# Storing the residual rows away to make room for a third gate and up buffer

## The reference

```
x = x + mix @ w_out                        # attention outputs, projected, added to the residual x
h = rms_norm(x, ln2)
# router: the best group of 8 experts by a softmax, in it the best 2 experts, two weights per token
y = sum over the token's two experts e of weight * (silu(h @ w_gate[e]) * (h @ w_up[e])) @ w_down[e]
x = x + y
out = rms_norm(x, ln_f)
```

## Time and profile before

| | |
|---|---|
| median of three runs | 2105.37 us |
| profiled execution, own time | 2101.73 us |
| its span in the trace | 2099.1 us |
| PE busy | 1821.9 us (87%) |
| DVE, ACT, POOL busy | 618.3, 474.5, 429.7 us |
| moved by DMA over the span | 527.22 MB, mean 251 GB/s |
| the chain that ended last, largest part | the load of `ht_region<-in_w_up`, 33% |

### The profile page before, as it was taken

How to read it: one execution, slowest core, us unless ns; L and a number is a source line. 1 busy time by engine, 2 the same in 40 slices (tenths; PEclk the granted TensorE clock), 3 DMA queues, 4 the chain that set the end, 5 groups by cost and what they waited for, 6 DMA issues and landing times. The chain is left out here.

```text
span 2099.1 us, 28102 instructions
## 1 busy us (share of the span) xinstructions
PE 1821.9 (87%) x11148; PEld 1276.7 (61%) x11148; DVE 618.3 (29%) x1464; ACT 474.5 (23%) x1008; POOL 429.7 (20%) x478
## 2 busy tenths in 40 slices
PE   6998999999999999999968888888888888888880
PEld 4877777777666666688845554555545555555550
DVE  4321224444666566601331111111111111111115
ACT  5222223323434443422301011011011110110102
POOL 2323333331000013244111111111111111111110
PEclk9999999999999999999979999999999999999995
DMA  9453223323221231143479999999999999999985
GB/s 277 119 137 102 63 79 81 77 64 79 53 51 41 71 121 41 41 152 101 168 316 424 425 427 425 425 425 426 426 425 424 426 425 425 423 424 422 421 352 243
DMA packets 190056, 527.22 MB, mean 251 GB/s; under 512 B 65650, under 2 KB 148850, under 8 KB 162074
## 3 DMA queue, kind: packets, MB, share of 16 engines
q1 hardware_dynamic: 171498, 509.18, 63.0%
q0 software_dynamic: 18480, 16.97, 2.4%
HBM read 530.38 MB, written 46.02 MB: 275 GB/s over the span
## 5 line engine op out<-in xcount | busy, mean ns | idle before, releaser
L873 PE MATMUL PJ<-ht_rounded,ring_rounded 128*128 128x512 f32 (+1 forms) x928 | 320.5, 399 | 4.9 <-ACT at_region L1267 4.9
L1150 PE MATMUL PJ<-at_region,ring_region 128*64 128x256 f32 x1024 | 263.6, 423 | 69.9 <-DMA at_region<-in_w_up 68.9
L1150 PE MATMUL PJ<-ht_region,ring_region 128*64 128x256 f32 x1024 | 236.3, 391 | 41.6 <-DMA ht_region<-in_w_up 41.6
L1151 PE MATMUL PJ<-at_region,ring_region 128*64 128x256 f32 x1024 | 264.3, 423 | 0.0
L1150 PEld LDWEIGHTS PJ<-at_region,ring_region 128*64 128x64 f32 x1024 | 154.0, 153 | 159.5 <-issue 101.5
L1151 PE MATMUL PJ<-ht_region,ring_region 128*64 128x256 f32 x1024 | 237.0, 391 | 0.0
L750 POOL TENSOR_TENSOR ring_rounded<-ring_region,ring_rounded 128x512 fp32r<-128x512 f32 x100 | 127.4, 1305 | 480.1 <-ACT ring_rounded L1212 480.1
L802 POOL DMA_INDIRECT y_scratch<-ring_region,s_idx x64 | 64.6, 1009 | 779.6 <-DVE ring_region L1824 765.2
L1150 PEld LDWEIGHTS PJ<-ht_region,ring_region 128*64 128x64 f32 x1024 | 142.0, 141 | 120.1 <-issue 70.9
L873 PEld LDWEIGHTS PJ<-ht_rounded,ring_rounded 128*128 128x128 f32 (+1 forms) x928 | 171.7, 189 | 53.7 <-issue 12.0
L1816 DVE TENSOR_TENSOR ring_region<-ring_region,PJ 64x256 f32<-64x256 f32 x64 | 27.1, 423 | 593.0 <-ACT ring_region L1419 593.0
(11 more groups left out here) (265 smaller groups left out, 2691.6 us busy)
## 6 DMA issues: line engine op xcount, KB each, us to landing
at_region<-in_w_gate SPq DMA_DIRECT2D x32, 2048.0 KB, 14.0
at_region<-in_w_down SPq DMA_DIRECT2D x32, 2048.0 KB, 21.5
at_region<-in_w_up SPq DMA_DIRECT2D x32, 2048.0 KB, 21.6
ht_region<-in_w_gate SPq DMA_DIRECT2D x32, 2048.0 KB, 15.4
ht_region<-in_w_up SPq DMA_DIRECT2D x32, 2048.0 KB, 22.8
x_region<-in_w_down SPq DMA_DIRECT2D x32, 2048.0 KB, 22.5
ring_region<-in_w_in SPq DMA_DIRECT2D x36, 1024.0 KB, 5.9
ring_region<-in_w_out SPq DMA_DIRECT2D x16, 1024.0 KB, 5.1
```

The source lines that it names most:

```text
L873: ins = mm(out, w[:, k, 0:width], h[:, k, :], start=k == 0 and i == 0, stop=k == KT - 1 and i == 2)
L1150: mm(GU[0:CAP, 0:D_EXPERT], x, gate[:, j, :], start=j == 0, stop=j == KT - 1)
L1151: ins = mm(GU[CAP:2 * CAP, 0:D_EXPERT], x, up[:, j, :], start=j == 0, stop=j == KT - 1)
```

## The change

Four things are done, all in the list that SP runs, with what the other engines must know of them.

- `x_sb` is stored to a new HBM scratch, one row tile of 1 MiB at a time, as soon as its last addition is done. The four stores stand ahead of `load_down(0, 0)` and the stores of h.
- MIX0 becomes a third gate and up buffer, used once: for expert 1, loaded after `load_up(0, 0)` and once x is stored. The HT0 buffer, which the logits free, takes gate and up of expert 2.
- From expert 3 on the two old buffers alternate as before, but with the parity exchanged: odd experts in AT0, even ones in HT0. The down buffers keep their parity. The loads of experts 3 and 4 are written out ahead of the loop.
- After the last weight load four loads bring x back into MIX0, and DVE waits for them (`x_again`) before the final additions.

PE's program takes the buffer and its count from `gate_up_place` and is otherwise the same. The passes after the first, which run only if an expert has more than 64 rows, keep the old scheme.

```diff
-        ex_w = [AT0 + 12 * KB, HT0]
+        ex_w = [AT0 + 12 * KB, HT0, MIX0]
...
-            sp.wait_ge(wo_ready, NT * NT)
+            for t in range(NT):
+                sp.wait_ge(wo_added, NT * (NT - 1) + t + 1)
+                sp.dma_start(x_dram[t * P:(t + 1) * P, :], x_sb[:, t, :]).then_inc(x_stored, 16)
             load_down(0, 0)
...
             load_up(0, 0)
+            sp.wait_ge(x_stored, 16 * NT)
+            load_gate(1, 2)
+            load_up(1, 2)
             sp.wait_ge(logits_ready, 1)
-            load_expert(1, 1)
+            load_down(1, 1)
+            load_gate(2, 1)
+            load_up(2, 1)
...
-            expert_loads(0)
+            for e in (3, 4):
+                sp.wait_ge(gu_done, 1 if e == 3 else 3)
+                load_gate(e, (e + 1) % 2)
+                load_up(e, (e + 1) % 2)
+                sp.wait_ge(down_done, e - 2)
+                load_down(e - 1, (e - 1) % 2)
+            sp.wait_ge(down_done, 3)
+            load_down(4, 0)
+            with sp.Fori(0, (E_ALL - 6) // 2) as i:
+                for b in range(2):
+                    sp.wait_ge(gu_done, i * 2 + (b + 4))
+                    nxt = bass.ds(i * 2 + (b + 5), 1)
...
+                    sp.wait_ge(down_done, i * 2 + (b + 4))
...
+            sp.wait_ge(gu_done, E_ALL - 2)
+            load_gate(E_ALL - 1, 0)
+            load_up(E_ALL - 1, 0)
+            sp.wait_ge(down_done, E_ALL - 2)
+            load_down(E_ALL - 1, 1)
+            for t in range(NT):
+                sp.dma_start(x_sb[:, t, :], x_dram[t * P:(t + 1) * P, :]).then_inc(x_again, 16)
...
+            def gate_up_place(c, i, b4, first):
+                if not first:
+                    return b4 % 2, c * PAIRS + i * 2 + (b4 // 2 - b4 % 2)
+                if b4 % 2 == 0:
+                    return 1, i * 2 + (b4 // 2 - 1)
+                return 0, i * 2 + b4 // 2
...
+                gu, held = place
...
-                pe.wait_ge(gu_in[b], k * 32 + 32)
+                pe.wait_ge(gu_in[gu], held * 32 + 32)
...
             dve.wait_ge(lnf_in, 16)
+            dve.wait_ge(x_again, 16 * NT)
```

More of the change, by code:

```diff
@@ L324, in hybrid_block_moe_kernel @@
         y_dram = nc.dram_tensor("y_scratch", [2 * T, D], F32, kind="Internal").ap()
+        x_dram = nc.dram_tensor("x_scratch", [T, D], F32, kind="Internal").ap()
         KB = 256
@@ L527, in hybrid_block_moe_kernel @@
         slot_of_ready, table_ready = sem("slot_of_ready"), sem("table_ready")
+        x_stored, x_again = sem("x_stored"), sem("x_again")
         xg_cleared, g_copied, s_copied = sem("xg_cleared"), sem("g_copied"), sem("s_copied")
@@ L530, in hybrid_block_moe_kernel @@
         scattered = [sem(f"scattered{b}") for b in range(RUN)]
-        gu_in = [sem(f"gu_in{b}") for b in range(2)]
+        gu_in = [sem(f"gu_in{b}") for b in range(3)]
         down_in = [sem(f"down_in{b}") for b in range(2)]
@@ L700, in expert_loads @@
                           .then_inc(down_in[b], 16)
-            expert_loads(0)
+            for e in (3, 4):
[10 more added lines that the diff above has]
+                    nxt = bass.ds(i * 2 + (b + 5), 1)
+                    sp.dma_start(ex_halves(b, 0), gate_rows[:, nxt]).then_inc(gu_in[b], 16)
+                    sp.dma_start(ex_halves(b, 1), up_rows[:, nxt]).then_inc(gu_in[b], 16)
+                    sp.wait_ge(down_done, i * 2 + (b + 4))
+                    sp.dma_start(ex_down[1 - b].rearrange("p k (a n) -> p a (k n)", a=1), down_rows[:, nxt, :])\
+                      .then_inc(down_in[1 - b], 16)
+            sp.wait_ge(gu_done, E_ALL - 2)
[5 more added lines that the diff above has]
+                sp.dma_start(x_sb[:, t, :], x_dram[t * P:(t + 1) * P, :]).then_inc(x_again, 16)
             sp.wait_ge(most_ready, 1)
@@ L1134, in turn_gathered, with expert @@
                 ins.then_inc(xg_transposed, 1)
-            def expert(c, i, b4, last):
+            def gate_up_place(c, i, b4, first):
[4 more added lines that the diff above has]
+                return 0, i * 2 + b4 // 2
+            def expert(c, i, b4, last, place):
                 e = c * E_ALL + i * RUN + b4
@@ L1140, in expert @@
                 Y = S[:, b, :, :]
-                gate = ex_gu[b][:, 0, :].rearrange("p (k n) -> p k n", k=KT)
-                up = ex_gu[b][:, 1, :].rearrange("p (k n) -> p k n", k=KT)
-                pe.wait_ge(gu_in[b], k * 32 + 32)
+                gu, held = place
+                gate = ex_gu[gu][:, 0, :].rearrange("p (k n) -> p k n", k=KT)
+                up = ex_gu[gu][:, 1, :].rearrange("p (k n) -> p k n", k=KT)
+                pe.wait_ge(gu_in[gu], held * 32 + 32)
                 pe.wait_ge(xT_a, e + 1)
@@ L1173, in expert, with expert_pass @@
                 ins.then_inc(down_done, 1)
-            def expert_pass(c):
+            def expert_pass(c, first):
                 turn_gathered(c * E_ALL, c * RUNS, 0)
                 for b4 in range(RUN):
-                    expert(c, 0, b4, False)
+                    expert(c, 0, b4, False, ((0, 0), (2, 0), (1, 0), (0, 1))[b4] if first else gate_up_place(c, 0, b4, first))
                 with pe.Fori(1, RUNS - 1) as i:
                     for b4 in range(RUN):
-                        expert(c, i, b4, False)
+                        expert(c, i, b4, False, gate_up_place(c, i, b4, first))
                 for b4 in range(RUN):
-                    expert(c, RUNS - 1, b4, b4 == RUN - 1)
+                    expert(c, RUNS - 1, b4, b4 == RUN - 1, gate_up_place(c, RUNS - 1, b4, first))
             pe.wait_ge(slots_ready, 1)
-            expert_pass(0)
+            expert_pass(0, True)
             pe.wait_ge(most_ready, 1)
@@ L1190, in _ @@
                 with pe.Fori(1, PASSES) as c:
-                    expert_pass(c)
+                    expert_pass(c, False)
             with pe.Else():
```

## The result

The changed kernel takes 2112.16 us, the median of ten runs (2110.42 to 2113.54), against 2105.11 us for the kernel before (ten runs, 2101.54 to 2108.39). The ratio is 1.0036, with a 95% interval from 1.0028 to 1.0045. So the change makes the kernel slower, by 7.05 us between the medians and by 7.6 us (6 to 9.5) as the ratio has it. The prediction was 2114 us and +10.5. The profiled executions have spans of 2099.1 and 2108.3 us, 9.2 us apart.

What follows compares the result with a forecast made beforehand. Weight loads were taken to bound the expert stage, at 5.18 us per 2 MiB load. The terms -0.6 + 0 + 10.1 + 1.0 = +10.5 us, on 2103.6, gave 2114 us, range 2109 to 2123.

Steps and rivals of the forecast that it cites:

- The first gather: Start of the expert stage: issued into a full DMA, it takes 13.2 us instead of 3.1, +10.1 us.
- The moved loads: Gate and up of expert 2 loaded ahead; a hole before gate 4 gives nearly all back: -0.6 us.
- Down 3 late: Expert 3's down load lands at about 1122.7, wanted at about 1119; PE loses up to 4 us, counted as 0.
- The stores of x: Before the expert stage: h stored near 1047 instead of 1041.2, covered by POOL's wait for the index list: 0 us.
- The end: Four loads bring x back behind down 63, disturbing at most the last microsecond before the last scatter: +1 us.
- The third rival: At the kernel's end x returns late, the last scatter takes 10.0 us, y loads start 7 us later: 2120; chance 0.10.
- the start: Time of the kernel before to which the sum is added: 2103.6 us, the middle of runs at 2101.5 and 2105.5.

Runs made afterwards that it cites:

- traffic alone: Kernel before plus two unused 2 MiB copies from HBM to HBM behind the loads of expert 1: 2115.89 us, ratio 1.0051.
- the hold: Changed kernel with SP holding gate and up of expert 2 back until the first gather has landed: 2108.25 us, ratio 1.0015 to the kernel before.
- taking x away: Changed kernel without any store or load back of x, so its output is wrong: 2112.59 us, ratio 1.0041 to the kernel before.
- down 3 early: Changed kernel with the load of down 3 issued ahead of the wait for the third products: 2107.2 us, ratio 1.0009 to the kernel before.
- the buffer in turn: Changed kernel with the third buffer used for experts 1, 4 and 7 instead of once: 2102.2 us, ratio 0.9985 to the kernel before.
- x alone: Kernel before with x stored and brought back, and no third buffer: 2107.12 us, ratio 1.0013.

## Why the prediction came out, and where its terms were off

- **The first gather, +10.1 forecast, +7.6 measured** (10.65 against 3.09 us, with the index list ready 0.5 us later). The mechanism is shown three ways: traffic alone makes the gather late, the hold takes 4.6 us of it back, and taking x away changes nothing. The size was off. I took the median of 13 gathers in the full stream; the second and the fourth gather of the changed kernel, issued at 1065.74 and 1069.86, did take 13.6 and 13.1 us, but the first took 10.65. It took 10.46, 10.68 and 10.50 in the three other kernels that had six loads in front of it. Why the first one is quicker than those behind it stays open. 0.8 us came back in expert 0's products, which took 8.9 us against 9.7, at a granted clock of 0.79 of full speed against 0.75.
- **The moved loads, -0.6 forecast, -0.6 measured**: products of expert 0 end 7.34 us late, up 63 lands 6.71 us late. From the issue of gate 4 at 1111.43 to the landing of up 6 at 1161.25 nine loads took 49.8 us, which is 9 of 5.18 and a start of 3.2, where 3.1 was assumed. Up 6 was then 6.8 us late, and so it stayed. With bounds of -2.2 to +0.3, the hit to a tenth is luck. The step on which this rests, that a third buffer used once gives its lead back in a hole before gate 4, is shown by the kernels with down 3 early and with the buffer in turn. The hole was forecast as about 7 us. The DMA share of 0.24 from 1104 to 1114 makes 7.6.
- **Down 3 late, 0 forecast.** In the chain of the changed kernel PE stands for 3.1 us from 1126.05, ahead of expert 3's down products. The trace names nothing that released it, but down 3 was issued only at 1112.28 behind two loads. Without x and with the hold PE stands as long at the same place (3.2 and 3.4 us), and with down 3 early it does not stand there at all, so down 3 was what it waited for. The stream behind was full, so nothing of this reached the end. That the load costs nothing by being late, but nearly its own 5 us by not being in the hole, I had not seen.
- **The stores of x, 0 on the path.** h was stored at 1045.99 (forecast 1047, before 1041.19), and POOL then still waited 12.84 us for the index list (17.09 in the earlier trace rows). In the changed kernel this holds but for the index list, which came 0.5 us later though the first addition began at the same time (1013.08 against 1013.02). In all seven kernels that store x it came 0.3 to 0.6 us later, counted from that addition, and in the two others not. What holds it up is not shown. As a statement on x alone the term was wrong: without the six loads in front, the same stores cost the gather 3.2 us, since they move the three loads behind them.
- **The end, +1 forecast, about +2.5 measured**, and at most a third of it from x. The last scatter took 3.36 us instead of 2.95, and with the issue of the y loads this makes 0.75. Even that is not surely x: the copies' kernel has 3.15 us without x, and the third buffer in turn 3.01 with it. The other 1.7 us are PE's clock (last section), for which the forecast had no term. The third rival (x holds the last scatter for 10 us) did not happen; the last tile of x was issued at 2031.4 and landed 29.9 us later, at 2061.3, 1.1 us ahead of that scatter. In the old times that is 2052.9, some 2 us sooner than the forecast's 2055.

The Trainium skill (DMA: Bandwidth & Descriptors, section Anatomy of one DMA — SWDGE (gpsimd) path) fits such a DMA as about 2.0 us plus its bytes at 436 GB/s, 3.2 us by estimate. In this case it holds for the gather of before (3.09), and for no first gather that was issued with some 6 us or more of loads still to land ahead of it (6.05 to 16.41).

The sum on the trace, 7.6 + 0.5 - 0.8 - 0.6 + 1.7 + 0.8, is the 9.2 us between the two spans. The medians lie 7.05 us apart. The profiled execution of before was one of its quick ones (2101.73 against a median of 2105.11), which the prediction had allowed for with a start of 2103.6.

So the mechanism that decided was right, and the number was better than its terms. The gather was put 2.5 us too high, the end 1.5 and the index list 0.5 too low, and the start 1.5 below the median; 2114 is 1.8 us off, while the forecast difference of +10.5 is 3.5 above the 7.05 measured. The range was also not worked out evenly: the 2 us for where the runs lie were taken off its lower end and not put onto its upper one, which by the same bounds is about 2125 and not 2123.

## What to carry to other kernels

Filling an idle stretch of DMA is only a gain if nothing small and urgent has to go through the same engines just then: look for the gather or the store that the whole chip waits for in that stretch, and let the bulk loads wait for it. A spare buffer that is used once is a lead that is paid back as soon as its turn would come again; keep it in turn until the stage is bound by DMA, after which two buffers are enough (with two, the DMA share is 1.01 from 1200 to 1400 us). And when loads wait in a plain list, check that none stands behind a wait that it does not need: here one line's place was worth 4.6 us of loads, more than half of the loss.

## What the runs showed of the hardware

**The first indirect gather beside bulk loads** landed right behind the last load issued ahead of it, or after some 10.5 us if that was sooner, where the loads go from HBM to on-chip memory. Before: last load in front at 1065.8, gather at 1066.1. With x alone 1071.5 and 1071.7, with the hold 1070.9 and 1071.1. With six loads, the last of which landed at 1080.1, the gather was there at 1074.2. Beside copies from HBM to HBM it took 16.4 us, until 1 us behind the last of them. The 10.5 us are four kernels' first gather and no limit for others: later ones of the changed kernel took 13.6 and 13.1 us.

**At the end of the kernel the same wait of PE sometimes cost 1.7 us of clock and sometimes nothing.** From the landing of up 63 to the issue of the last scatter it takes, in the ten traces, either 14.34 to 14.35 us (before, x alone, the two with the buffer in turn, the two with down 3 early) or 16.03 to 16.04 (the changed kernel, without x, the hold, the copies). PE's longest wait for this landing, in the traces of before, of the changed kernel and of the one with down 3 early (us in total, times, longest):

```profile
PE PJ L1150 <- DMA ht_region<-in_w_up: 0.3, 1, 0.3
```

```profile
PE PJ L1192 <- DMA at_region<-in_w_up: 2.8, 2, 2.0
```

```profile
PE PJ L1196 <- DMA at_region<-in_w_up: 2.0, 1, 2.0
```

And the stretches: before from the landing to the products' end; then of the changed kernel the wait, the first 4 us of the products and the rest; then with down 3 early the wait and the first 4 us:

```profile
2039.70:2046.90 7.20, 7.13 (x64) 4.51 (x64) 0.47 (x1) 0.38 (x1) 1.17 (x2) 1.00 0.12 47
```

```profile
2044.50:2046.40 1.90, 0.00 (x0) 0.00 (x0) 0.68 (x1) 0.58 (x1) 0.28 (x1) 1.00 0.99 414
2046.40:2050.40 4.00, 3.94 (x22) 2.30 (x24) 0.00 (x0) 0.00 (x0) 0.90 (x2) 0.57 1.01 421
2050.40:2055.30 4.90, 4.88 (x46) 2.98 (x42) 0.00 (x0) 0.00 (x0) 0.00 (x0) 1.00 0.66 270
```

```profile
2040.77:2042.77 2.00, 0.01 (x2) 0.00 (x0) 0.69 (x1) 0.60 (x1) 0.30 (x1) 1.00 1.03 434
2042.77:2046.77 4.00, 3.96 (x38) 2.66 (x40) 0.00 (x0) 0.00 (x0) 0.88 (x2) 1.00 1.00 420
```

After 0.3 us of waiting the 64 products ran in 7.2 us at the full 2.4 GHz. After 1.9 us in the changed kernel the granted clock was 0.57 for 4 us, near the level of 1.2 GHz, then full again, and they took 8.9 us. But a wait of 1.9 to 2.1 us for this landing stands in eight of the ten traces. In four of them the clock fell behind it to 0.57 to 0.60, and in the other four (the buffer in turn and down 3 early, each with and without the hold) it stayed at 1.00. So the length of the wait does not decide it, and what does stays open. Nor is it known whether a kernel keeps one form from execution to execution, since each was traced once. The 1.7 us in the trace of the changed kernel are thus not shown to belong to the change. Inside the stage such a fall is hidden, since the next load is what PE waits for. At the last expert it is not.
